# Four sequence pairs moved into the steps of the prompt attention in a two-layer hybrid decoder step

## The chip, the cores and the metric

One launch of one program on one core of a Trainium2 chip. The metric is the device time of one execution, from the first to the last instruction and what lies around it, in microseconds (us). The engines are TensorE (PE, with its weight loads PEld), VectorE (DVE), ScalarE (ACT), GpSimd (POOL) and SyncE (SP), which only issues transfers here. Each engine works through its own queue in program order; they meet at semaphores. All arithmetic around this change is f32, which PE does in two instructions per product.

## The reference, cut to what matters

A two-layer decoder handles a prompt (512 tokens) and eight short sample sequences (8 tokens each) with the same weights. In each layer the normed input goes through one projection into three head groups: RG-LRU, MLA (attention over a compressed latent) and GLA. Each group's output is normed by itself, the three are concatenated, multiplied by `w_out` and added to the input; a mixture of experts follows. The prompt attends to itself; each sample sequence attends to 1024 cached positions, kept in 8 pages of 128, and to its own 8 tokens:

```
past_ckv = cache_ckv[l][page_table].reshape(nb, -1, KV_RANK)       # 128 columns
past_kpe = cache_kpe[l][page_table].reshape(nb, -1, QK_ROPE)       # 32 columns
s = (einsum('bqhr,bkr->bhqk', qa, ckv) + einsum('bqhr,bkr->bhqk', qp, kpe)) * scale
p = softmax(where(k_pos <= q_pos, s, -inf))
o = einsum('bhqk,bkr->bqhr', p, ckv)
...
merged = concatenate([rmsnorm(out_a, n_a), rmsnorm(out_b, n_b), rmsnorm(out_c, n_c)], axis=-1)
return merged @ lw['w_out'], ...
```

## The kernel before, in words

Every engine has a program of its own in one block; loops over layers and steps are unrolled in Python, and the five programs are written so that their queues fit together. PSUM has eight banks; `psum_plan` lists every use of a bank in PE's order, and the uses go round the eight banks in turn. `begin` makes PE wait until the use eight places earlier has been read, `take` makes a reader wait until the bank is full, `give` marks it read and `after` waits for that mark.

**The prompt attention** runs in `ATT_STEPS` = 35 steps, one per head and query tile (8 x 4), with three more to drain. In a step PE makes the scores of tile `s`, transposes the probabilities of tile `s - 2` (`pt`), and every eighth step multiplies a pair of heads with the values (`pv`) and spreads their reciprocal sums (`rs`). DVE takes the maximum of the scores, ACT the exponential and the copies of the transposes. In the same steps the GLA group runs: five state products (`delta`, steps 0 to 6), the products between chunks (`inter`, step 7), and 16 offset sums (`dp` and `ds`, steps 8 to 24), whose factors DVE multiplies and whose results it adds up. At step 26 (`GN_STEP`) follow the sums of the GLA norm, and at step 27 DVE finishes the GLA output (`out_c`, L1335 to L1340).

**The sample attention** takes the eight sequences in four pairs, each on 128 rows (2 sequences x 8 heads x 8 tokens). A pair has three pieces in PE's queue. `sample_scores` (L1662, L1666, L1671) makes the scores over 1088 columns in three banks (`ss`); DVE takes the maximum (`sample_max`, L1286) and ACT the exponentials (`sample_exp`, L875); DVE divides by the sum over all 1088 columns (`sample_divide`, L1295). `sample_values` transposes the probabilities (L1682, L1684; banks `sp`), waits for ACT's three copies (L882, L885) and multiplies them with the cached latent (L1692, L1695; bank `sv`). `sample_turn` (L1701) transposes the copied result (`svt`), which ACT puts into `qas`. Pair 0 has its pieces in steps 27, 30 and 33. Pairs 1 to 3 follow after the last step in the order of `SAMPLE_ORDER`. When all four are turned, PE multiplies by `w_uv` (`uvs`, L1798).

**The pages.** SP loads them (L486 to L503). For each pair it reads sixteen page numbers into registers, then issues one transfer of 192 KB a page: per partition 128 latent columns, 128 transposed ones and 128 for the transposed rotary key, of which only 32 partitions hold data. There are two buffers in `rg`. Pair 0's load waits for `inter` and for the GLA states to be stored, pair 1's for `out_c`, whose inputs lie under its buffer, and pairs 2 and 3 for the values of pair 0 and 1. The halves of `w_out` are issued on the same queue between them.

**The norm of the groups** follows `out_b`, the mark that the MLA output is complete: ACT squares the eight 128-row pieces of the three groups (L967), PE sums them over partitions with a matrix of ones (`osum`, L1807), ACT makes the reciprocal roots through Ln and Exp (`rstds`, L758 and L761, a table load each), and DVE multiplies (L1355, `merged`). The output projection (`wo`, L1818) takes the eight pieces in order; DVE adds its result to `x` (L1361). Norm, router and the experts (L1858 to L1887) follow. SP loads the first expert's weights after the merge (L514, L518).

The functions, with their lines:

Of the kernel before, what the change touches and what calls it, by code (L numbers as in the profile page):

```python
# [17 lines left out]
ALU = mybir.AluOpType  # L18
ACT = mybir.ActivationFunctionType
# [3 lines left out]
P = 128  # L23
# [30 lines left out]
ATT_STEPS = HEADS * 4 + 3  # L54
# [90 lines left out]
def psum_plan():  # L145
# [19 lines left out]
    for s in range(ATT_STEPS):  # L165
# [9 lines left out]
        if s == SAMPLE_STEP:  # L175
            keys += [("ss", 0, k) for k in range(3)]
        if s == SAMPLE_STEP + 3:
            keys += [("sp", 0, k) for k in range(3)] + [("sv", 0)]
        if s == SAMPLE_STEP + 6:
            keys += [("svt", 0)]  # L180
# [7 lines left out]
    for kind, p in SAMPLE_ORDER:  # L188
        keys += {"scores": [("ss", p, k) for k in range(3)],
                 "values": [("sp", p, k) for k in range(3)] + [("sv", p)], "turn": [("svt", p)]}[kind]  # L190
    keys += [("uvs",)]
    keys += [("osum", k, h) for k in range(3) for h in range(2)]
# [7 lines left out]
def hybrid_step(nc, a, o):  # L200
# [5 lines left out]
    with ExitStack() as ctx:  # L206
# [36 lines left out]
        def cut(region, at, *dims):  # L243
# [14 lines left out]
        wout = [cut(rb, 0, KT, 512), cut(ra, 0, KT, 512)]  # L258
# [19 lines left out]
        spread = cut(rb, 1152, SEQ)  # L278
# [30 lines left out]
        pg = [cut(rg, 6144 * k, 2, NPAGE, 3 * P) for k in (1, 0)]  # L309
        CKV, CKVT, KPET = slice(0, P), slice(P, 2 * P), slice(2 * P, 3 * P)  # L310
        sprob = cut(re, 8960, 1088)
        spT = cut(re, 10048, 9, P)
        osq = cut(rg, 0, 8, T)
        ors = cut(rg, 4608, 3, T)
# [17 lines left out]
            gmsk_ready kt_ready diff_ready exp_ready w_ready gn_ready out_c max_ready rs_ready s_max s_prob  # L332
# [6 lines left out]
        page_in = [sem(f"page{k}_in") for k in range(2)]  # L339
        wout_in = [sem(f"wout{k}_in") for k in range(2)]  # L340
# [101 lines left out]
        def _(sp):  # L442
# [16 lines left out]
            for L in range(DEPTH):  # L459
# [60 lines left out]
                sp.wait_ge(S["merged"], 8 * (L + 1))  # L520
# [209 lines left out]
        def _(act):  # L730
# [62 lines left out]
            for L in range(DEPTH):  # L793
# [77 lines left out]
                def sample_exp(p):  # L871
                    act.wait_ge(S["s_max"], 4 * L + p + 1)
                    for k, (at, n) in enumerate(((0, 512), (512, 512), (1024, NS))):
                        bk = take(act, L, ("ss", p, k))
                        give(fn(sprob[:, at:at + n], bk[:, 0:n], ACT.Exp, bias=sm[:, 84:85],  # L875
                                accum_out=sm[:, 85 + k:86 + k]), ("ss", p, k))

                def probabilities_out(p):
                    for k in range(3):
# [4 lines left out]
                        else:  # L884
                            give(copy(spT[:NS, 8, :], bk[:NS, 0:P]), ("sp", p, k))  # L885

                def sample_rows(p):
                    bk = take(act, L, ("sv", p))
                    give(copy(svs[:, p % 2, :], bk[:, 0:P]), ("sv", p))
# [4 lines left out]

                for s in range(ATT_STEPS):
# [26 lines left out]
                    if s == 1:  # L923
# [6 lines left out]
                        for e in range(2):  # L930
                            bk = take(act, L, ("qp", e))
                            give(copy(qp[0:ROPE, :, :].rearrange("p b (h e q) -> p e h b q", e=2, q=NQ)[:, e],
# [7 lines left out]
                    if s == SAMPLE_STEP + 1:  # L940
                        sample_exp(0)
# [1052 lines left out]
```

## Time and profile before

| | |
|---|---|
| median of 3 runs | 1611.6 us (1609.57 to 1612.38) |
| the profiled execution | 1611.4 us |
| its span | 1609.5 us |
| mean granted TensorE clock | 0.888 |
| PE busy | 1275.7 us, 79% |
| DVE, ACT, POOL busy | 545.7, 359.1, 320.8 us |
| HBM read, written | 289.96, 27.09 MB |

Rows are read so. A timeline row has its start and length in us, the engine, the line, the operation, what it writes and reads, and how many instructions are merged in it; brackets hold idle time before it and what ended it.
### The profile page before, as it was taken

To read this page: it belongs to the slowest core of one execution; us is meant where nothing else is said; L and a number is where in the kernel's file an instruction comes from. 1 tells how busy PE (TensorE), PEld (TensorE's weight loads), DVE (VectorE), ACT (ScalarE), POOL (GpSimd) and SP (SyncE) were. 2 spreads that over 40 slices of the span, in tenths; PEclk is the share of its full clock that TensorE was granted. 3 is DMA by queue.
4 is the path that set the end of the run, shared out by engine and by line. 5 is a ranking of instruction groups with operands and counts; after the bars stand their busy time and mean duration, and the time that the engine had idled before them with its cause. 6 is when DMAs were issued, how large, how long until landed. Compare 5 with 4: busy or idle time off the path is not lost.

```text
span 1609.5 us, 21838 instructions
## 1 busy us (share of the span) xinstructions
PE 1275.7 (79%) x7203; PEld 767.7 (48%) x7204; DVE 545.7 (34%) x1345; ACT 359.1 (22%) x823; POOL 320.8 (20%) x729
## 2 busy tenths in 40 slices
PE   5999977769956887778499997866898477888881
PEld 4777555434453443444277765533446244444440
DVE  2275685102243111111516557731113411111115
ACT  4233336121111101111314333522311011011112
POOL 0012410000002333333102052000000133333440
PEclk9999999669957999999699999975897599999996
DMA  5310021442094889995521002064207499978745
GB/s 211 99 36 27 9 80 45 165 144 78 40 385 168 344 348 400 408 407 227 197 97 63 27 0 88 1 205 136 92 13 286 175 381 408 377 275 344 292 174 182
DMA packets 98900, 299.11 MB, mean 186 GB/s; under 512 B 13230, under 2 KB 29966, under 8 KB 98450
## 3 DMA queue, kind: packets, MB, share of 16 engines
q1 hardware_dynamic: 85426, 273.21, 45.3%
q0 software_dynamic: 13408, 25.04, 4.3%
q8 instruction: 39, 0.64, 0.2%
q14 instruction: 27, 0.22, 0.0%
HBM read 289.96 MB, written 27.09 MB: 197 GB/s over the span
## 4 chain that ended last, share of the span: by engine, by line
PE 52%; DMA 22%; DVE 11%; issue 6%; SPq 4%; ACT 2%; POOL 2%; POOLq 1%; DVEq 0%; ACTq 0%
DMA ra<-h_rows,slot_now 19%; PE bank L1542 14%; PE bank L1818 9%; PE bank L1876 5%; PE bank L1887 3%; PE bank L1858 3%; SPq L495 2%; PE bank L1831 2%; PE bank L1574 2%; DVE rg L1262 1%; PE bank L1740 1%; PE bank L1662 1%; PE bank L1666 1%; PE bank L1807 1%; DVE rf L1259 1%
## 5 line engine op out<-in xcount | busy, mean ns | idle before, releaser
L1542 PE MATMUL bank<-ra,rb 128*128 128x288 f32 (+1 forms) x896 | 225.2, 414 | 1.9 <-ACT ra L736 1.9
L1542 PEld LDWEIGHTS bank<-ra,rb 128*128 128x128 f32 (+1 forms) x896 | 170.4, 191 | 54.0 <-issue 3.6
L1477 DVE COPY rb<-bank 128x512 f32<-128x512 f32 x71 | 49.1, 692 | 223.0 <-DMA y_rows<-rb,home_now 158.1
L990 ACT ACTIVATE rb<-bank 128x128 f32<-128x128 f32 x71 | 19.7, 278 | 417.9 <-PE bank L1876 417.9
L1858 PE MATMUL bank<-cst,ra 128*128 128x128 f32 x292 | 49.7, 295 | 74.3 <-DMA ra<-h_rows,slot_now 74.2
L1876 PE MATMUL bank<-rg,rb 128*64 128x256 f32 x768 | 92.3, 395 | 8.0 <-issue 5.2
L1887 PE MATMUL bank<-re,rb 128*64 128x512 f32 x296 | 81.5, 677 | 14.2 <-DVE rb L1473 14.2
L1471 DVE TENSOR_TENSOR rb<-rb,bank 128x128 f32<-128x128 f32 x71 | 20.4, 288 | 196.8 <-ACT rb L990 196.8
L1876 PE MATMUL bank<-re,rb 128*64 128x256 f32 x736 | 84.8, 383 | 2.5 <-issue 0.8
L697 POOL DMA_INDIRECT ra<-h_rows,slot_now x73 | 77.1, 1056 | 39.7 <-issue 39.7
L1876 PEld LDWEIGHTS bank<-rg,rb 128*64 128x64 f32 x768 | 56.7, 142 | 53.2 <-issue 29.2
L1858 PEld LDWEIGHTS bank<-cst,ra 128*128 128x128 f32 x292 | 31.8, 145 | 105.3 <-DMA ra<-h_rows,slot_now 98.0
L686 POOL DMA_INDIRECT y_rows<-rb,home_now x71 | 73.0, 1029 | 38.8 <-issue 38.8
L1876 PEld LDWEIGHTS bank<-re,rb 128*64 128x64 f32 x736 | 53.1, 138 | 44.6 <-issue 22.6
L982 ACT COPY rb<-bank 128x512 f32<-128x512 f32 x73 | 42.8, 586 | 140.0 <-PE bank L1858 140.0
L671 POOL DMA_DIRECT2D h_rows<-re x4 | 2.2, 550 | 353.8 <-DVE re L1008 353.8
L1740 PE MATMUL bank<-re 128*128 128x128 f32 (+3 forms) x128 | 52.1, 490 | 9.4 <-DVE rf L1259 6.8
L1887 PE MATMUL bank<-rg,rb 128*64 128x512 f32 x192 | 48.2, 624 | 9.2 <-DVE rb L1473 9.2
L1876 PE MATMUL bank<-rf,rb 128*64 128x256 f32 x448 | 51.3, 382 | 1.4 <-issue 1.2
L1361 DVE TENSOR_TENSOR x<-x,bank 128x512 f32<-128x512 f32 (+1 forms) x20 | 13.7, 686 | 109.9 <-PE bank L1818 109.9
L918 ACT ACTIVATE re<-bank,sm 128x128 f32<-128x128 f32 (+1 forms) x64 | 33.9, 530 | 73.9 <-DVE sm L1303 73.6
L1637 PE MATMUL bank<-re,cst 128*128 128x512 f32 (+15 forms) x128 | 40.5, 434 | 11.6 <-DVE rf L1259 6.3
(354 smaller groups left out, 2055.6 us busy)
## 6 DMA issues: line engine op xcount, KB each, us to landing
rg<-in_w_moe SPq DMA_DIRECT2D x24, 2048.0 KB, 11.3
re<-in_w_moe SPq DMA_DIRECT2D x20, 2048.0 KB, 13.0
re<-in_w_moe SPq DMA_DIRECT2D x30, 1024.0 KB, 15.0
rg<-in_cache SPq DMA_DIRECT2D x128, 192.0 KB, 3.5
rg<-in_w_moe SPq DMA_DIRECT2D x24, 1024.0 KB, 13.7
rf<-in_w_moe SPq DMA_DIRECT2D x10, 2048.0 KB, 12.4
ra<-in_w_moe SPq DMA_DIRECT2D x10, 2048.0 KB, 13.4
rb<-in_win SPq DMA_DIRECT2D x28, 512.0 KB, 3.8
```

Of the source, the lines that this page charges most:

```text
L686: nc.gpsimd.indirect_dma_start(y_halves, bass.IndirectOffsetOnAxis(ap=home_now[:, 0:1], axis=0), ysb, None, bounds_check=4 * T - 1, oob_is ...
L697: nc.gpsimd.indirect_dma_start(xg, None, h_halves, bass.IndirectOffsetOnAxis(ap=slot_now[:, 0:1], axis=0), bounds_check=2 * T - 1, oob_is_ ...
L918: give(fn(prob[:, s % 2, 0:n], bk[:, 0:n], ACT.Exp, bias=peaks[:, s % 16:s % 16 + 1], accum_out=sums[:, s % 16:s % 16 + 1]), key)
L982: copy(xT, bank[0][:, :].rearrange("p (k h n) -> p k h n", k=4, h=2)).then_inc(S["xt_ready"], 1)
L1477: V.tensor_copy(ysb, bank[5][:, :]).then_inc(S["y_ready"], 1)
L1542: ins = mm(bk[:mrows, 0:HALF], win[:, n % 4, k, :mrows], hT[:, k, cols], start=k == 0, stop=k == KT - 1)
L1637: done(mm(bk[:, 0:n], cst[:, C_BM + j * P:C_BM + (j + 1) * P], gw[:, d % 2, 0:n], start=True, stop=True), ("dp", d, j))
L1740: mm(bk[:, 0:n], qt[:, hd, i * P:n], kt[:, hd, 0:n], start=True, stop=False)
L1818: ins = mm(bk[:r, :], merged[k][:, t * P:t * P + r], wout[n][:, k, :], start=k == 0, stop=k == 7)
L1858: ins = tr(bank[0][:, k * P:(k + 1) * P], xg[:, k * P:(k + 1) * P], ident)
L1876: ins = mm(bank[2][SLOTS * h:SLOTS * (h + 1), 0:DE], xT[:, k % 4, k // 4, :], wgu[s][:, k, h * DE:(h + 1) * DE], start=k == 0, stop=k == K ...
L1887: ins = mm(bank[5][SLOTS * n:SLOTS * (n + 1), :], actT[:, k, :], wdn[s][:, k, 512 * n:512 * n + 512], start=k == 0, stop=k == 1)
```

## The change

All four pairs run inside the steps, now 36: scores at steps 14, 19, 24 and 29, values three steps later, the turn six steps later. The exponentials are no longer divided; DVE multiplies the 128 columns of the `sv` bank by the reciprocal sum instead (ACT copied them before). A page is 128 KB (latent and transposed latent) with the rotary key as a second transfer of 16 KB into `kpg`, pair `p` on partitions 32p to 32p + 31; `qp` is made on all 128 partitions so that the scores can use those rows. The buffers lie over other memory: pair 0 and 2 in `rg`, 1 and 3 in `rb`, and pair 1 no longer waits for `out_c`. `w_out`'s first half goes to `rg` after `out_c`, and the first expert's load after the fifth output tile. The RG-LRU and GLA groups are squared at step 30, summed at 31, their roots taken at 32 and multiplied at 33; the MLA group alone is normed after `out_b`. The output projection takes pieces 0, 1, 6, 7 first.

```
-ATT_STEPS = HEADS * 4 + 3
+ATT_STEPS = HEADS * 4 + 4
-SAMPLE_STEP = 27
-SAMPLE_ORDER = (("scores", 1), ("scores", 2), ("values", 1), ("values", 2), ("turn", 1), ("turn", 2),
-                ("scores", 3), ("values", 3), ("turn", 3))
+SAMPLE_AT = (14, 19, 24, 29)
+EARLY_STEP = 30
+MERGE_ORDER = (0, 1, 6, 7, 2, 3, 4, 5)
+NORM_GROUPS = {0: (0, 2, 256), 2: (2, 4, 256), 1: (4, 8, 512)}
...
-        wout = [cut(rb, 0, KT, 512), cut(ra, 0, KT, 512)]
+        wout = [cut(rg, 0, KT, 512), cut(ra, 0, KT, 512)]
-        spread = cut(rb, 1152, SEQ)
+        spread = cut(re, 13568, SEQ)
-        pg = [cut(rg, 6144 * k, 2, NPAGE, 3 * P) for k in (1, 0)]
-        sprob = cut(re, 8960, 1088)
-        spT = cut(re, 10048, 9, P)
-        osq = cut(rg, 0, 8, T)
-        ors = cut(rg, 4608, 3, T)
+        pg = [cut(rg, 4096, 2, NPAGE, 2 * P), cut(rb, 0, 2, NPAGE, 2 * P)]
+        kpg = cut(rg, 8192, 2, NPAGE, P)
+        sprob, sprob_new = cut(rg, 10240, 1024), cut(re, 2944, NS)
+        spT, spT_new = cut(rg, 11264, 8, P), cut(re, 3008, P)
+        osq = cut(rg, 4096, 8, T)
+        ors = cut(re, 8960, 3, T)
...
 SP
-                take(sp, L, ("inter", 2))
-                sp.wait_ge(S["gla_out"], 32 * (L + 1))
                 for p in range(4):
                     page = [sp.value_load(pages[0:1, col:col + 1], ...) for col in ...]
-                    if p == 1:
-                        sp.wait_ge(S["out_c"], L + 1)
+                    if p == 0:
+                        take(sp, L, ("inter", 2))
+                        sp.wait_ge(S["gla_out"], 32 * (L + 1))
                     if p > 1:
                         take(sp, L, ("sv", p - 2))
                     for n in range(2 * NPAGE):
                         sp.dma_start(pg[p % 2][:, n // NPAGE, n % NPAGE, :], a["cache"][...])
-                    if p == 2:
-                        after(sp, L, ("pv", 3))
-                        sp.dma_start(wout[0], wo_rows[:, :, 0:512]).then_inc(wout_in[0], 16)
-                    if p == 3:
-                        take(sp, L, ("pv", 3))
-                        sp.dma_start(wout[1], wo_rows[:, :, 512:1024]).then_inc(wout_in[1], 16)
+                        sp.dma_start(kpg[ROPE * p:ROPE * (p + 1), n // NPAGE, n % NPAGE, :], a["cache_kpe"][...])
+                sp.wait_ge(S["out_c"], L + 1)
+                sp.dma_start(wout[0], wo_rows[:, :, 0:512]).then_inc(wout_in[0], 16)
+                take(sp, L, ("pv", 3))
+                sp.dma_start(wout[1], wo_rows[:, :, 512:1024]).then_inc(wout_in[1], 16)
...
-                sp.wait_ge(S["merged"], 8 * (L + 1))
+                take(sp, L, ("wo", 0, TT - 1))
                 load_gate_up(0, 0)
...
 ACT
+                    for p, at in enumerate(SAMPLE_AT):
+                        if s == at + 1:
+                            if p == 0:
+                                act.wait_ge(S["gla_out"], 32 * (L + 1))
+                            sample_exp(p)
+                        if s == at + 3:
+                            probabilities_out(p)
+                        if s == at + 6:
+                            sample_out(p)
+                    if s == EARLY_STEP:
+                        act.wait_ge(S["out_c"], L + 1)
+                        for p in range(3):
+                            take(act, L, ("sv", p))
+                        squares(range(0, 4))
+                    if s == EARLY_STEP + 2:
+                        group_rstds(0, 2)
...
-                for k in range(8):
-                    fn(osq[:, k, :], merged[k], ACT.Square).then_inc(S["osq_ready"], 1)
-                rstds(L, *[(("osum", k, h), ors[:, k, cols], n, "ors_ready")
-                           for k, n in enumerate((256, 512, 256)) for h, cols in enumerate(halves)])
+                squares(range(4, 8))
+                group_rstds(1)
...
 DVE
-                    link(V.reciprocal(sm[:, 89:90], sm[:, 88:89]))
-                    V.tensor_scalar(sprob, sprob, sm[:, 89:90], None, ALU.mult).then_inc(S["s_prob"], 1)
+                    V.reciprocal(sm[:, 89:90], sm[:, 88:89]).then_inc(S["s_sums"], 1)
+                def sample_rows(p):
+                    bk = take(dve, L, ("sv", p))
+                    dve.wait_ge(S["s_sums"], 4 * L + p + 1)
+                    give(V.tensor_scalar(svs[:, p % 2, :], bk[:, 0:P], sm[:, 89:90], None, ALU.mult), ("sv", p))
+                def normed_groups(slots, ready):
+                    dve.wait_ge(S["ors_ready"], 6 * L + ready)
+                    for n in slots:
+                        k, g = MERGE_ORDER[n], (0, 0, 2, 2, 1, 1, 1, 1)[n]
+                        V.scalar_tensor_tensor(merged[k], ...).then_inc(S["merged"], 1)
...
+                        if s == at: sample_max(p)
+                        if s == at + 1: sample_divide(p)
+                        if s == at + 4: sample_rows(p)
+                    if s == EARLY_STEP + 3:
+                        normed_groups(range(0, 4), 4)
...
 PE
+                    pe.wait_ge(kpage_in[p % 2], 16 * 2 * NPAGE * (2 * L + p // 2 + 1))
+                    rows = slice(ROPE * p, ROPE * (p + 1))
-                            ins = mm(bk[64 * b2:64 * b2 + 64, 0:n], qp[0:32, 2 * p + b2, :],
-                                     pg[p % 2][0:32, b2, 4 * k:4 * k + 4, KPET] if k < 2 else kpeT[0:32, SEQ:T],
+                            ins = mm(bk[64 * b2:64 * b2 + 64, 0:n], qp[rows, 2 * p + b2, :],
+                                     kpg[rows, b2, 4 * k:4 * k + 4, :] if k < 2 else kpeT[rows, SEQ:T],
-                    pe.wait_ge(S["s_prob"], 4 * L + p + 1)
+                    for k in range(3):
+                        after(pe, L, ("ss", p, k))
...
+                        if s == at: sample_scores(p)
+                        if s == at + 3: sample_values(p)
+                        if s == at + 6: sample_turn(p)
...
+                    if s == EARLY_STEP + 1:
+                        for g in (0, 2):
+                            group_sums(g)
...
+                group_sums(1)
...
-                        for k in range(8):
+                        for i, k in enumerate(MERGE_ORDER):
                             if n == 0 and t == 0:
-                                pe.wait_ge(S["merged"], 8 * L + k + 1)
+                                pe.wait_ge(S["merged"], 8 * L + i + 1)
```

## Rows read from the trace of the kernel before

**Rows 1.** Windows, layer 0: steps 14 to 34, pairs 1 to 3, group norm.
```profile
224.80:292.50 67.70, 53.24 (x398) 37.30 (x400) 40.84 (x120) 32.88 (x89) 3.52 (x8) 0.90 0.15 48
292.50:354.80 62.30, 40.19 (x222) 19.88 (x218) 9.28 (x22) 11.27 (x34) 0.00 (x0) 0.62 0.51 169
354.80:372.10 17.30, 11.69 (x48) 8.41 (x48) 1.47 (x4) 11.85 (x22) 0.00 (x0) 0.80 0.09 31
```

**Rows 2.** Waits, 170 to 372 us: engine, line, releaser, total us, times, longest.
```profile
PE bank L1662 <- DMA rg<-in_cache: 15.0, 2, 7.8
```

**Rows 3.** Line L495, both layers: issue ns min/median/max, waits for it, landing.
```profile
L495 SPq DMA_DIRECT2D rg<-in_cache x128: 332/333/1891, 202.3 to 1105.8; - x128
...
  PE bank L1662: 29.2, 4
...
DMA to landing us min/median/max: 2.3/3.5/6.1
```

**Rows 4.** Timeline, layer 0: last `rs`, last turn, `uvs`.
```profile
291.74 1.07 PE L1752 MATMUL bank<-cst,sm 128*64 128x128 f32 x16
...
353.99 0.33 PE L1701 MATMUL bank<-cst,rf 128*128 128x128 f32 x1 [0.37 <-ACT rf L889]
...
354.87 0.69 PE L1798 MATMUL bank<-re 128*64 128x64 f32 x16 [0.56 <-ACT re L893]
```

**Rows 5.** Timeline: pair 0's scores, an exponential, pair 2's transposes and values.
```profile
264.53 1.08 PE L1662 MATMUL bank<-rg,re 128*64 128x512 f32 x4
...
269.08 0.22 PE L1671 MATMUL bank<-mask 128*64 128x64 bf16 x2
...
297.86 0.69 ACT L875 ACTIVATE re<-bank,sm 128x512 f32<-128x512 f32 x1 [4.42 <-DVE sm L1288]
...
321.00 1.87 PE L1682 MATMUL bank<-cst,re 128*128 128x128 f32 x8
...
325.80 0.44 PE L1695 MATMUL bank<-re 64*64 64x128 f32 x4
```

**Rows 6.** Timeline: step 29's scores, GLA output, pair 0's values.
```profile
269.95 0.60 PE L1740 MATMUL bank<-re 128*128 128x256 f32 x2
...
272.90 1.36 DVE L1340 SCALAR_TENSOR_TENSOR rf<-rf,rg 128x1152 f32<-128x1152 f32 x1
...
278.02 1.97 PE L1682 MATMUL bank<-cst,re 128*128 128x128 f32 x8 [1.81 <-DVE re L1295]
...
284.65 0.63 PE L1695 MATMUL bank<-re 64*64 64x128 f32 x4
```

**Rows 7.** Windows of PE alone: busy, granted clock, DMA share, GB/s.
```profile
282.00:285.00 3.00, 3.00 (x30) 0.50 0.93 294
```

**Rows 8.** Timeline, layer 0: `out_b`, group norm, first output product and its add.
```profile
356.06 0.15 DVE L1349 COPY sm<-sm 128x1 f32<-128x1 f32 x1
...
360.95 1.28 ACT L758 ACT_TABLE_LOAD   x1
...
371.21 1.55 DVE L1355 SCALAR_TENSOR_TENSOR rf<-rf,vec,rg 128x576 f32<-128x576 f32 x2 [15.00 <-ACT rg L761]
...
373.96 3.60 PE L1818 MATMUL bank<-rb,re 128*128 128x512 f32 x8
...
379.32 0.69 DVE L1361 TENSOR_TENSOR x<-x,bank 128x512 f32<-128x512 f32 x1 [2.19 <-PE bank L1818]
```

**Rows 9.** The chain that ended last: start, us, engine and line.
```profile
35.98 39.00 PE bank L1542 x160
```

**Rows 10.** Timeline: `inter`, then the issues of pairs 0 and 1, and 2.
```profile
187.75 4.84 PE L1629 MATMUL bank<-rg 128*64 128x32 f32 x160
...
202.31 80.98 SPq L495 DMA_DIRECT2D rg<-in_cache  x32
...
292.28 9.27 SPq L495 DMA_DIRECT2D rg<-in_cache  x16
```

**Rows 11.** Timeline: the first expert's first products, layer 0.
```profile
500.13 5.13 PE L1876 MATMUL bank<-rg,rb 128*64 128x256 f32 x30 [0.86 <-ACT rb L982]
```

More of the change, by code:

```diff
@@ L187, in psum_plan @@
             keys += [("gnorm", j, h) for j in range(2) for h in range(2)]
[L188 to L190 removed]
+        if s == EARLY_STEP + 1:
+            keys += [("osum", g, h) for g in (0, 2) for h in range(2)]
     keys += [("uvs",)]
[L192 removed]
+    keys += [("osum", 1, h) for h in range(2)]
     keys += [("wo", n, t) for n in range(2) for t in range(TT)]
@@ L872, in sample_exp @@
                     act.wait_ge(S["s_max"], 4 * L + p + 1)
-                    for k, (at, n) in enumerate(((0, 512), (512, 512), (1024, NS))):
+                    for k, dst in enumerate((sprob[:, 0:512], sprob[:, 512:1024], sprob_new)):
                         bk = take(act, L, ("ss", p, k))
-                        give(fn(sprob[:, at:at + n], bk[:, 0:n], ACT.Exp, bias=sm[:, 84:85],
+                        give(fn(dst, bk[:, 0:512 if k < 2 else NS], ACT.Exp, bias=sm[:, 84:85],
                                 accum_out=sm[:, 85 + k:86 + k]), ("ss", p, k))
@@ L884, in probabilities_out @@
                         else:
[L885 to L889, printed above, removed]
+                            give(copy(spT_new[:NS, :], bk[:NS, 0:P]), ("sp", p, k))
                 def sample_out(p):
@@ L893, in sample_out, with squares, group_rstds @@
                     give(copy(qas[:, 2 * p:2 * p + 2, :], bk[:, 0:P].rearrange("p (b c) -> p b c", b=2)), ("svt", p))
+                def squares(slots):
+                    for n in slots:
+                        fn(osq[:, n, :], merged[MERGE_ORDER[n]], ACT.Square).then_inc(S["osq_ready"], 1)
+                def group_rstds(*groups):
+                    rstds(L, *[(("osum", g, h), ors[:, g, cols], NORM_GROUPS[g][2], "ors_ready")
+                               for g in groups for h, cols in enumerate(halves)])
                 for s in range(ATT_STEPS):
@@ L1721, in sample_queries, with group_sums @@
                         for n in range(4):
-                            ins = mm(bk[0:ROPE, n * NS:(n + 1) * NS], sel[rows, 0:ROPE], qt[rows, 2 * n + e, SEQ:T],
+                            ins = mm(bk[:, n * NS:(n + 1) * NS], sel[rows, :], qt[rows, 2 * n + e, SEQ:T],
                                      start=True, stop=True)
                         done(ins, ("qp", e))
+                def group_sums(g):
+                    n0, n1, _ = NORM_GROUPS[g]
+                    pe.wait_ge(S["osq_ready"], 8 * L + n1)
+                    for h, cols in enumerate(halves):
+                        bk = begin(pe, L, ("osum", g, h))
+                        for n in range(n0, n1):
+                            ins = mm(bk[:, 0:HALF], ones, osq[:, n, cols], start=n == n0, stop=n == n1 - 1)
+                        done(ins, ("osum", g, h))
                 pe.wait_ge(S["uv_in"], 16 * (L + 1))
@@ L1789, in _ @@
                         gla_norm_sums()
-                for kind, p in SAMPLE_ORDER:
-                    {"scores": sample_scores, "values": sample_values, "turn": sample_turn}[kind](p)
+                    if s == EARLY_STEP + 1:
+                        for g in (0, 2):
+                            group_sums(g)
                 for p in range(4):
@@ L1800, in _ @@
                 done(ins, ("uvs",))
-                for g, (k0, k1) in enumerate(((0, 2), (2, 6), (6, 8))):
-                    pe.wait_ge(S["osq_ready"], 8 * L + k1)
-                    for h, cols in enumerate(halves):
-                        bk = begin(pe, L, ("osum", g, h))
-                        for k in range(k0, k1):
-                            ins = mm(bk[:, 0:HALF], ones, osq[:, k, cols], start=k == k0, stop=k == k1 - 1)
-                        done(ins, ("osum", g, h))
+                group_sums(1)
                 for n in range(2):
```

106 lines of the change are left out of this document (44 added, 62 removed).

## The prediction, before the changed kernel ran

> **What bounds the kernel now.** I read the page's slices first: TensorE is busy nearly everywhere, but in a stretch near 300 us, and again in the second layer, its granted clock drops well below full. The windows by stage say why [rows 1]. The prompt attention's steps 14 to 34 (224.8 to 292.5 us) keep PE 53.2 of 67.7 us busy at 0.90. The next 62.3 us, in which sequence pairs 1 to 3 run one after another, have 40.2 us of PE at a clock of 0.62, that is, mostly at 1.2 GHz. The 17.3 us after them are the norm of the three head groups. Together that is 80 us a layer in which the reader should see no engine full. The waits name the two ends: PE stands 15.0 us for cache pages in two waits [rows 2], and the line that issues the pages has four such waits over both layers, 29.2 us, so the second layer behaves as the first [rows 3]. The rest of the stretch is each pair's own chain (scores, maximum, exponentials, transposes, copies, values, turn) with nothing beside it.
>
> I work on layer 0 and double it. The execution profiled took 1611.4 us (span 1609.5); the median of the runs is 1611.6, so I subtract from 1611.4.
>
> **What leaves.** From the end of the last `rs` product (291.74 + 1.07 = 292.81) to the start of `uvs` (354.87) there are 62.1 us [rows 4]. Afterwards only pair 3's turn, its copy and the hand-over stay there: 353.99 to 354.87, 0.9 us. So 61.2 us leave.
>
> **What enters the steps.** A pair's price on PE at 2.4 GHz: scores 264.53 to 269.30, 4.8 us; transposes, three ACT copies and values 321.00 to 326.24, 5.2 us; the turn 0.3 [rows 5]. That is 10.3 us, all in PE's queue, since `sample_values` waits for its copies where it stands. Pairs 0 and 1 whole and pair 2's scores come ahead of step 27: 2 x 10.3 + 4.8 = 25.4. After it come the rest of pair 2 (5.5) and pair 3 (10.3); pair 0, which stood there, goes: 4.8 for its scores, 278.02 to 285.28 for its values [rows 6] and 0.3, 12.4 in all. Net 25.4 + 15.8 - 12.4 = 28.8.
>
> Two corrections of opposite sign I take as equal. PE is idle 14.5 us in the stretch [rows 1], mostly waiting for DVE's GLA sums, and can swallow some of the pair work. Against that, a step with scores uses seven or eight of the eight PSUM banks, so the next step's offset sums wait until ACT has read the three score banks, behind that step's prompt exponential; ACT needs 0.7 us for a 512-column one [rows 5] and the read of its sum, some 2 us for three, once per pair. DVE gets three maxima of the same columns, about as long, in steps where it is the fullest engine; its normalising of `sprob` leaves, and a small scaled copy of the `sv` bank comes. Bounds: all of the idle time absorbed, less 4 us of such waits, -10; every moved pair at its price in the tail, (62.1 - 15.0) / 3 = 15.7 instead of 10.3, +16. I stay at the PE price, because the queue is in order and the row is of the same instructions.
>
> The early norm adds on PE four matmul pairs for each of two groups. 160 matmul instructions of the same 288 columns take 39.0 us, 0.244 each [rows 9]; a product is two of them, so 8 products are 3.9 us. On ACT four squares, two table loads, four Ln and four Exp stand ahead of the copy of `pt` 31, for which the last `pv` waits: I charge 3.3 us of wait (0 if PE's own values of pair 3 cover it, 8 if they cover none). Steps in all: 28.8 + 3.9 + 3.3 = 36.0.
>
> The table load's row shows 1.28 us [rows 8]. The Trainium skill (ScalarE: Activation LUTs, What ACT_TABLE_LOAD costs) counts a drain with each switch, about 2.66 us together; the change adds two switches a layer, so by that rule it would be up to 2.8 us a layer more and 1560 us in the end. The eight squares before the load run from 356.21 to 360.95, 0.59 each, which leaves no visible drain; I go by the row.
>
> **The tail.** From `out_b` (356.06 + 0.15) to DVE's first add after the first output product (379.32) are 23.1 us [rows 8]. After the change: four squares 2.4 (0.59 each); the sums of group 1, 16 instructions at 0.244, 3.9 [rows 9]; an Ln, a table load of 1.28 and two Exp, together some 2.7; one DVE product 0.8 (two in 1.55). Meanwhile PE does the four products of the early groups (0.9 each from eight instructions in 3.60) in its queue behind the sums, and after DVE's first product has the other four left: 3.6. Sum 13.4, so 9.7 leave.
>
> Per layer at full clock: -61.2 + 36.0 - 9.7 = -34.9.
>
> **The clock.** Before, PE stopped while DVE made the GLA norm (272.90 + 1.36), and the values that followed at 278.02 ran at 1.2 GHz [rows 6, 7]. That DVE work and ACT's table loads stay at steps 26 and 27, so the stop stays, and now pair 2's values and perhaps pair 3's scores follow it: 2 us, or 6 with the scores. A second such stop is likely at the end, where PE waits for ACT's early norm, then for `out_b`: pv, rs and the group sums at half clock cost up to 7. I take 3 + 3. Net -28.9 per layer, -58 for both: 1611.4 - 58 = 1553.6, **1554 us**.
>
> **Edits that I cost at nothing.** SP: pair 0's sixteen page numbers are now read ahead of the wait for `inter`, so issues start near 192.6 rather than 202.31 [rows 10]. A pair now takes 32 issues instead of 16. One issue takes 0.33 us of SP [rows 3], 16 in a row 9.27 us, 0.58 each, paced by the data [rows 10]; reading 16 page numbers 9.7 us (192.59 to 202.31). At 0.58, the upper end, pair 1's pages are issued by 239.5, pair 2's by 267.8 and pair 3's by 296.1, plus 3.5 to land [rows 3]: 299.6. Pair 3's scores stand in step 29, at 269.95 before [rows 6]; ahead of them come 25.4 and pair 2's values (5.2), less pair 0's old scores (4.8), and what the clock and the waits add: 296 to 302. So it is close at that pace, and well early at 0.40, where pair 3's issue waits for pair 1's values instead. A late pair would hold in PE's queue all prompt steps from 29 on. `out_c`, `wout` and the gain come after on SP: `wout[0]` now waits for `out_c`, not for `pv` 3, and is there before the output product. The first expert's load waits for the fifth output tile instead of the merge, some 15 us later against the stage; its first reader starts at 500.13 [rows 11], over 100 us on; nothing if that cover stays. The other expert loads follow the same point as before. The other new waits are met when they come: ACT's at step 30 for `out_c` and `sv` 0 to 2 (PE made `sv` 2 three steps earlier; behind it stand the copies of `pt` 29 on, for which PE would wait), ACT's for `gla_out` at step 15 and DVE's for its own reciprocal. Page bytes fall from 192 to 144 KB. Moving `spread`, `sprob`, `osq` and `ors`, and `qp` on 128 partitions, change no operation's length.
>
> **Rivals.** *The idle time takes it in.* If the DVE-bound steps swallow the pairs to the lower bound and the clock holds: -34.9 - 10 + 2 = -43 a layer, 1525. For it: 14.5 us of PE idle. Against: in-order waits within a step, at every pair. *The pairs cost in the steps what they cost in the tail* (15.7 each, half clock after each wait): -34.9 + 16 + 6 = -13 a layer, 1586. For it: pair 0's values took 7.3 us within the steps [rows 6]. Against: that was after the norm's stop alone. *SP becomes the bound, slower than before.* Pair 3's pages land at 192.6 + 128 c + 3 x 9.7 + 3.5 for c us an issue; at c = 0.60 PE begins to wait, and at 0.82 the whole gain of 28.9 is gone; at 1.0, 1656. For it: the longest single issue took 1.89 us [rows 3]. Against: the median of 0.33, and 0.58 with larger transfers. The Trainium skill (DMA: Bandwidth & Descriptors, Bandwidth) speaks against splitting: it calls transfers under 64 KB descriptor-dominated, and its table gives 0.68 us at 4 KB and 0.95 at 64 KB; with about 0.8 for the 16 KB ones and 0.4 for the pages, c would be some 0.6, an estimate, at the edge of that loss. No row here shows a 16 KB load. *Nothing moves:* the steps stretch by all that the tail loses; only with both upper bounds at once.
>
> **Chances.** The forecast, 1544 to 1570, has 0.50; the first rival, below 1544, 0.24; the second, 1570 to 1600, 0.18; SP 0.05; no change 0.03. A measurement of this kernel tells 0.2% (3 us) from no change, so faster 0.92, same 0.03, slower 0.05. From 1530 to 1586 about 0.8 lie.
>
> **What would show it.** Right: no DMA releaser for the scores; `uvs` about 1.2 us after the last turn's start; step 27's first score 25 us after its old place; the last `rs` near 329 to 335; the first DVE add after the output product near 350; the clock at 0.5 after the GLA norm. Wrong, towards slower: PE waiting for `in_cache` ahead of pair 3's scores, or SP's 32 issues taking over 19 us. Wrong, towards faster: steps 14 to 26 stretched by under 18 us.

## The result, and the profile after

The changed kernel took 1566.2 us (median of four runs), the kernel before 1612.0 beside it: ratio 0.972, 95% interval 0.967 to 0.977. That is 46 us faster; the prediction was 1554, so 58 faster. The four times lie on two levels, 1560 and 1572, and the execution profiled (1572.1, span 1570.2, 39.3 below the span before) is one of the upper ones. In a later group of runs the same kernel took 1577.7 beside 1610.5 (`after_again` below), 33 us faster, so the size of the gain is known only as some 33 to 46 us.

The forecast of the prediction, per layer, was -28.9. From the start of `inter` (187.75 before [rows 10], 187.06 after) to the first add of the output product (379.32 [rows 8], 359.14) the way is 191.6 us before and 172.1 after in layer 0, 191.4 and 172.1 in layer 1: 19.4 us a layer are saved, 9.5 fewer than forecast. All that the change moved lies in this way, since two layers of it make 38.8 of the 39.3 us.

First, the windows of the stages, answering to [rows 1]: the steps up to step 27, the other steps with what is left of the pairs, and the group norm (columns: stretch, length, busy time of PE, its weight loads, DVE, ACT, POOL, granted clock, DMA share, GB/s).

```profile
224.10:300.20 76.10, 60.70 (x409) 36.93 (x410) 37.66 (x121) 26.95 (x79) 3.57 (x8) 0.87 0.31 87
300.20:339.80 39.60, 28.07 (x225) 19.49 (x223) 12.96 (x24) 22.04 (x53) 0.00 (x0) 0.91 0.15 54
339.80:355.40 15.60, 11.58 (x43) 7.10 (x41) 2.14 (x5) 7.50 (x12) 0.00 (x0) 0.78 0.48 169
```

The 62 us at a clock of 0.62 are gone. What stays is PE's own work at about 0.9, with stops in it. PE's waits from `inter` to the first add no longer name a DMA, in either layer; three of the longest (engine, line, releaser: us, times, longest) are the copies of a pair's probabilities, the squares of the early norm and DVE's read of a pair's values:

```profile
PE bank L1703 <- ACT re L888: 8.0, 3, 4.4
PE bank L1743 <- ACT rg L897: 6.1, 2, 3.1
...
PE bank L1645 <- DVE rf L1298: 3.4, 1, 3.4
```

The steps up to step 27, in PE's timeline (start, length, engine, line, operation, idle before it and its releaser), with step 27's first score last. In the kernel before that score stood at 263.30:

```profile
263.30 1.02 PE L1740 MATMUL bank<-re 128*128 128x512 f32 x2
```

In the changed kernel:

```profile
256.94 0.59 PE L1645 MATMUL bank<-re,cst 128*128 128x192 f32 x2 [3.40 <-DVE rf L1298]
...
278.10 0.55 PE L1766 MATMUL bank<-cst,re 128*128 128x128 f32 x3 [1.57 <-DVE rf L1298]
...
278.64 1.50 PE L1672 MATMUL bank<-rg,re 128*64 128x512 f32 x4
...
280.07 1.97 PE L1676 MATMUL bank<-rg,re 32*64 32x512 f32 x4
...
300.18 1.02 PE L1760 MATMUL bank<-re 128*128 128x512 f32 x2
```

L1298 is `sample_rows`, which the change moved from ACT to DVE, last in DVE's step. PE stands 3.40 us for it in step 18 (in the kernel before, 1.52 us at that place, for an offset product) and 1.57 us in step 24. Right behind the second stop pair 2's scores run at 1.97 us for four products instead of 1.08. The windows of PE alone show it as the clock (length, busy, granted clock, DMA share, GB/s):

```profile
276.00:279.00 3.00, 1.43 (x10) 1.00 0.49 135
279.00:282.00 3.00, 3.00 (x10) 0.53 0.50 145
...
288.00:291.00 3.00, 2.04 (x8) 0.50 0.44 129
```

Then the end of the layer's attention: pair 2's values behind the GLA norm, pair 3's scores, the early sums, the values of pair 3, the last `rs`, `uvs`, the last group's sums, and on DVE `out_b` and the first add.

```profile
306.87 3.42 PE L1703 MATMUL bank<-rg 128*64 128x128 f32 x32 [4.40 <-ACT re L888]
312.32 1.08 PE L1672 MATMUL bank<-rb,re 128*64 128x512 f32 x4
322.35 5.84 PE L1743 MATMUL bank<-rg,cst 128*128 128x288 f32 x16 [2.99 <-ACT rg L897]
332.17 1.97 PE L1703 MATMUL bank<-rb,rg 128*64 128x128 f32 x32 [2.67 <-ACT re L761]
338.77 1.07 PE L1772 MATMUL bank<-cst,sm 128*64 128x128 f32 x16
340.88 0.69 PE L1819 MATMUL bank<-re 128*64 128x64 f32 x16 [0.79 <-ACT re L892]
...
342.06 0.15 DVE L1361 COPY sm<-sm 128x1 f32<-128x1 f32 x1
344.70 7.17 PE L1743 MATMUL bank<-rg,cst 128*128 128x288 f32 x16 [3.13 <-ACT rg L897]
...
359.14 0.69 DVE L1369 TENSOR_TENSOR x<-x,bank 128x512 f32<-128x512 f32 x1 [1.60 <-PE bank L1833]
```

And SP: the first issues of pair 3's pages, and its last. Issues follow each other by 0.52 us in the median, whether they carry 128 KB (L497) or 16 KB (L500). The last is out 21 us before pair 3's scores.

```profile
274.75 0.33 SPq L497 DMA_DIRECT2D rb<-in_cache  x1
275.27 0.33 SPq L500 DMA_DIRECT2D rg<-in_cache_kpe  x1
...
291.10 0.33 SPq L500 DMA_DIRECT2D rg<-in_cache_kpe  x1
```

### The profile page after: what moved, and what is told of

It reads as the page before. It is cut to its first block, busy times and chain, and to the rows that moved or that the text cites. A ratio compares the mean times of both kernels' runs of the same rounds, so it can differ in the third digit from the quotient of the medians.

```text
span 1570.2 us, 22262 instructions
## 1 busy us (share of the span) xinstructions
PE 1257.3 (80%) x7203; PEld 762.4 (49%) x7204; DVE 542.6 (35%) x1345; ACT 359.2 (23%) x819; POOL 320.4 (20%) x729
## 4 chain that ended last, share of the span: by engine, by line
PE 55%; DMA 22%; DVE 9%; issue 6%; ACT 5%; POOL 2%; POOLq 1%; SPq 0%; DVEq 0%; ACTq 0%
DMA ra<-h_rows,slot_now 20%; PE bank L1550 14%; PE bank L1833 8%; PE bank L1891 5%; PE bank L1873 3%; PE bank L1902 3%; PE bank L1760 2%; PE bank L1846 2%; PE bank L1582 2%; PE bank L1743 2%; PE bank L1676 1%; PE bank L1672 1%; PE bank L1782 1%; PE bank L1645 1%; DVE x L1492 1%
## 5 line engine op out<-in xcount | busy, mean ns | idle before, releaser
L989 ACT ACTIVATE rb<-bank 128x128 f32<-128x128 f32 x71 | 19.7, 277 | 413.5 <-PE bank L1891 413.5
L1479 DVE TENSOR_TENSOR rb<-rb,bank 128x128 f32<-128x128 f32 x71 | 20.5, 288 | 200.7 <-ACT rb L989 200.7
L1902 PE MATMUL bank<-re,rb 128*64 128x512 f32 x296 | 76.1, 637 | 14.2 <-DVE rb L1481 14.2
L1645 PE MATMUL bank<-re,cst 128*128 128x512 f32 (+15 forms) x128 | 44.0, 465 | 17.5 <-DVE rf L1298 6.8
L1313 DVE TENSOR_REDUCE sm<-bank 128x1 f32<-128x128 f32 (+1 forms) x64 | 31.0, 489 | 56.3 <-PE bank L1761 55.6
```

Of the source, the lines that this page charges most:

```text
L1645: done(mm(bk[:, 0:n], cst[:, C_BM + j * P:C_BM + (j + 1) * P], gw[:, d % 2, 0:n], start=True, stop=True), ("dp", d, j))
L1902: ins = mm(bank[5][SLOTS * n:SLOTS * (n + 1), :], actT[:, k, :], wdn[s][:, k, 512 * n:512 * n + 512], start=k == 0, stop=k == 1)
```

## The experiments

Twelve runs in four groups of kernels; the kernels of a group ran on one chip beside the kernel before (1610 to 1611 us each time). Times are medians of four runs (five for `rows_late_norm`).

| kernel | us | ratio to before, 95% |
|---|---|---|
| after_again | 1577.7 | 0.9785 to 0.9825 |
| rows_first | 1551.2 | 0.9620 to 0.9672 |
| late_norm | 1569.2 | 0.9693 to 0.9803 |
| split_pages | 1671.3 | 1.0332 to 1.0395 |
| rows_again | 1553.5 | 0.9630 to 0.9662 |
| rows_late_norm | 1550.5 | 0.9603 to 0.9635 |
| rows_two_in_tail | 1546.5 | 0.9578 to 0.9611 |
| rows_at_23_28 | 1557.8 | 0.9647 to 0.9693 |
| two_again | 1547.5 | 0.9597 to 0.9629 |
| three_in_tail | 1598.8 | 0.9917 to 0.9954 |
| tail_early_sums | 1552.0 | 0.9610 to 0.9646 |
| pair1_read_first | 1564.2 | 0.9647 to 0.9750 |

### after_again: the changed kernel once more

> The changed kernel once more, unchanged. Theory (the clock): the two levels of its time, 1560 and 1572 us, are executions in which TensorE keeps or loses its clock during pair 2's scores, steps 24 to 27. Times again near 1560 or 1572; in an execution near 1560 the eight long products of pair 2's scores take 1.08 us instead of 1.98 us in at least one layer, and steps 24 to 27 take 18 to 20 us there instead of 24.2. Rival: the levels come from somewhere else (the expert stages), and steps 24 to 27 take 24 us in either.

All four times were 1576 to 1581, above both levels expected, so no execution near 1560 came with a profile, and where the two levels differ could not be read directly. The interval of this run does not meet that of the first (0.967 to 0.977): the same kernel differs by 0.9% between them, and why is not shown. In the profile pair 2's scores are at half speed in both layers again (the two big score banks start at 281.23 and 284.56 in layer 0, 3.3 us apart where 2.0 is full clock). It serves as the base of the next three.

### rows_first: DVE reads the pair's values early in its step

```diff
+                    if s - 4 in SAMPLE_AT:
+                        sample_rows(SAMPLE_AT.index(s - 4))
                     if s > 0 and s % 8 == 0:
...
-                        if s == at + 4:
-                            sample_rows(p)
```

> VectorE scales and reads a pair's values (the bank sv) right after the step's maximum, ahead of the product with the row sums and the GLA offset. Theory (bank waits): the offset sums of step 18 wait 3.40 us, and a transpose of step 24 1.57 us, for this read alone; both waits go, some 5 us a layer, so 1556 us, and where the waits also took the clock in pair 2's scores, up to 12 us more (1544). Rival: the step's end was set by ScalarE's copies and exponentials anyway, so PE waits the same time for them: within 3 us of the changed kernel (1560 to 1572).

1551.2 us, 26.5 below the changed kernel on the same chip (15 below its first result). The rival is refuted. Of the two waits the first became 1.53 us (for an offset product's read of its own bank, as in the kernel before), the second 0.16. Pair 2's scores keep full clock:

```profile
256.25 1.13 PE L1760 MATMUL bank<-re 128*128 128x512 f32 x2 [1.53 <-DVE rf L1258]
...
275.68 0.55 PE L1766 MATMUL bank<-cst,re 128*128 128x128 f32 x3 [0.16 <-DVE rf L1298]
276.31 1.08 PE L1672 MATMUL bank<-rg,re 128*64 128x512 f32 x4
...
291.23 1.02 PE L1760 MATMUL bank<-re 128*128 128x512 f32 x2
```

```profile
279.00:282.00 3.00, 3.00 (x23) 1.00 0.53 146
```

Step 27's first score comes at 291.23 instead of 300.18; with `inter` 0.94 later here, that is 9.9 us in layer 0. The waits themselves account for 3.4 + 1.6 - 1.5 - 0.2 = 3.3 of it, so the larger part is the clock behind them: from `inter` to that score PE was busy 90.9 us in the changed kernel and 83.2 us here, with the same work.

### late_norm and rows_late_norm: the early norm undone

```diff
-                    if s == EARLY_STEP:
...
-                        squares(range(0, 4))
-                    if s == EARLY_STEP + 2:
-                        group_rstds(0, 2)
...
-                squares(range(4, 8))
-                group_rstds(1)
+                squares(range(0, 8))
+                group_rstds(0, 2, 1)
```

(PE's sums and DVE's products likewise go behind `out_b`.)

> The two early head groups are squared, summed and normed after out_b again, with the third. Theory of the prediction: the steps lose 3.9 us of sums and 3.3 us of waits for ScalarE, and the stretch from out_b to the first add grows from 16.9 us (as traced) by 9.7 us; net 2.5 us a layer slower, 1571 us. Rival: the early norm costs more than it gives, since in the trace it shows 5.84 us of sums and 2.99 + 2.67 us of waits against a gain of 23.1 - 16.9 = 6.2 us; then 5.3 us a layer faster, 1556 us.

1569.2 us, but with runs from 1563 to 1580 against 1576 to 1581 for its base: too wide to price 5 us. So it was made again on `rows_first`, where the clock in the steps is steady.

> rows_first with the two early head groups normed after out_b, with the third: the price of the early norm where the clock is steady. By the prediction's terms (7.2 us of sums and waits in the steps, 9.7 us taken from the tail) it is 2.5 us a layer slower than rows_first, 1556 us. Rival: the early norm costs PE 3.0 + 5.7 + 2.7 = 11.4 us in the steps, as rows_first's trace has them, and gives 6 to 7 us in the tail: 4 to 5 us a layer faster, 1542 us.

1550.5 beside 1553.5: neither the 5 us slower of the prediction nor the 9 us faster of the rival; the intervals overlap. The traces show why. These are the last `rs` products, `out_b` and the first add with the early norm (`rows_again`):

```profile
333.87 1.07 PE L1772 MATMUL bank<-cst,sm 128*64 128x128 f32 x16
...
337.16 0.15 DVE L1361 COPY sm<-sm 128x1 f32<-128x1 f32 x1
...
352.67 0.69 DVE L1369 TENSOR_TENSOR x<-x,bank 128x512 f32<-128x512 f32 x1 [1.61 <-PE bank L1833]
```

and without it (`rows_late_norm`, where `inter` stood 0.11 us earlier):

```profile
326.59 1.07 PE L1762 MATMUL bank<-cst,sm 128*64 128x128 f32 x16
...
329.88 0.15 DVE L1350 COPY sm<-sm 128x1 f32<-128x1 f32 x1
...
352.29 0.69 DVE L1359 TENSOR_TENSOR x<-x,bank 128x512 f32<-128x512 f32 x1 [3.63 <-PE bank L1821]
```

In layer 0 the early norm holds the last `rs` up by 7.2 us and shortens the way from `out_b` to the add by 22.4 - 15.5 = 6.9 us; in layer 1 the two are 8.6 and 6.9. It is worth nothing, within what these runs can tell.

### split_pages: twice as many issues for the same bytes

```diff
-                        sp.dma_start(pg[p % 2][:, n // NPAGE, n % NPAGE, :], ...
...
+                        for c in range(2):
+                            sp.dma_start(pg[p % 2][:, n // NPAGE, n % NPAGE, c * P:(c + 1) * P], ...
...
+                            sp.dma_start(kpg[ROPE * p + 16 * c:ROPE * p + 16 * c + 16, ...
```

> Every page transfer is cut into two, so 64 issues on SP for each pair instead of 32; the bytes are the same. Theory (the issues themselves cost 0.52 us each, whatever they carry): a pair's pages take 33 us, the last of pair 3's is issued near 353 us instead of 291 and its scores wait 40 us for it: 80 us more in two layers, 1640 to 1656 us (the prediction's own price for 1.0 us an issue was 1656). Rival: the cadence is set by what a transfer carries, half the bytes take half the time, nothing waits: 1560 to 1572 us.

1671.3 us, 94 above its base, somewhat over the theory's 80. The starts of pair 0's 64 issues run from 195.36 to 229.46, 0.54 us apart (0.52 in the median) with half the bytes: the cadence belongs to the issue. PE then waits for the pages of pairs 1, 2 and 3, and the scores behind each wait are at half clock, which the theory had not counted:

```profile
PE bank L1673 <- DMA rg<-in_cache_kpe: 32.0, 3, 16.7
```

```profile
319.38 1.97 PE L1673 MATMUL bank<-rg,re 128*64 128x512 f32 x4 [16.72 <-DMA rg<-in_cache_kpe]
```

So the prediction's slower rival is a real mechanism, with a price near its own (1656 at 1.0 us an issue of the change; two issues of 0.54 are 1.08), but the change stays clear of it at 0.52.

### rows_again, rows_two_in_tail, two_again: does the place of the pairs matter?

> rows_first once more, as the base of the three kernels beside it. Theory: without VectorE's late read TensorE keeps its clock through steps 24 to 27 in every execution, so the time stays near 1551 us (1549 to 1557) and shows no level 12 us apart. Rival: the clock falls there in some executions all the same, and times near 1565 us appear.

1552.3 to 1555.1 in four runs, one level.

```diff
-SAMPLE_AT = (14, 19, 24, 29)
+SAMPLE_AT = (14, 19)
+TAIL_ORDER = (("scores", 2), ("scores", 3), ("values", 2), ("values", 3), ("turn", 2), ("turn", 3))
```

> rows_late_norm with pairs 2 and 3 behind the last step, interleaved as the kernel before had its pairs 1 and 2; their pages lie ready long before. By the prediction's prices (10.3 us a pair in the steps, 15.7 us in the tail) two pairs moved out are 10.8 us a layer slower than rows_late_norm: 22 us more, 1564 to 1578 us. Rival (a pair costs in the steps what it costs in the tail): within 4 us of rows_late_norm. Rival (idle time absorbs part of a pair in the steps): more than 30 us slower.

1546.5 us, 4 below `rows_late_norm`. The prediction's prices (22 us slower) are refuted, and with them the idea that idle time in the steps absorbs a pair; the first rival, the same cost in either place, holds. The same kernel once more:

> rows_two_in_tail once more, as the base of the two kernels beside it: 1544 to 1549 us if its gain over the kernels with all pairs in the steps holds, 1550 us and more if it was chance.

1547.5, ratio 0.9613 against 0.9619 for `rows_late_norm` and 0.9646 for `rows_again`: the same as with all pairs in the steps and the norm late, or a few us better. In two_again's trace the two pairs run between the last `rs` and `uvs` in 19.7 us, at full clock (the two rows, then the window):

```profile
301.22 1.07 PE L1779 MATMUL bank<-cst,sm 128*64 128x128 f32 x16
...
321.67 0.69 PE L1826 MATMUL bank<-re 128*64 128x64 f32 x16 [0.56 <-ACT re L894]
```

```profile
302.00:321.70 19.70, 16.97 (x152) 8.66 (x149) 5.32 (x15) 6.94 (x21) 0.00 (x0) 1.00 0.31 108
```

That is 9.8 us a pair, behind the steps, with nothing beside them but each other. The prediction had 15.7 for this place, a mean over the kernel before, where the pairs ran at 0.62.

### three_in_tail: the wait for pages brought back

```diff
-SAMPLE_AT = (14, 19)
-TAIL_ORDER = (("scores", 2), ("scores", 3), ("values", 2), ("values", 3), ("turn", 2), ("turn", 3))
+SAMPLE_AT = (14,)
+TAIL_ORDER = (("scores", 1), ("scores", 2), ("values", 1), ("values", 2), ("turn", 1), ("turn", 2),
+              ("scores", 3), ("values", 3), ("turn", 3))
```

> rows_two_in_tail with pair 1 behind the last step too, in the order that the kernel before had. Theory (what the change removed is the wait for pages and its clock, not the place): with two page buffers pair 3's pages are asked for when pair 1's values are done, in the tail; 32 issues of 0.52 us and 2 us of landing, less 5 us of pair 2's values and turns, leave PE waiting 12 to 15 us, and pair 3's scores then run at half clock, 4 to 6 us longer: 16 to 21 us a layer more, 1578 to 1589 us. Rival (pairs simply cost more in the tail, or less): a move of one pair at 10.2 us for 10.3 us, within 4 us of rows_two_in_tail, or 5.4 us a layer slower (1557 us) by the prediction's prices.

1598.8 us, 51.3 above its base (`two_again`): the theory's mechanism, larger than it said. Only one pair went to another place, at a like price of its own, but its values now come in the tail, so pair 3's pages are asked for there. The wait equals the sum of the two in the kernel before [rows 2], and all of pair 3 behind it runs at 1.2 GHz (waits, then the windows of wait and pair):

```profile
PE bank L1686 <- DMA rb<-in_cache: 15.0, 1, 15.0
```

```profile
312.00:326.80 14.80, 0.00 (x0) 0.03 (x1) 0.00 (x0) 0.15 (x1) 0.00 (x0) 0.62 0.49 133
326.80:346.70 19.90, 15.63 (x72) 7.40 (x72) 2.43 (x7) 3.34 (x10) 0.00 (x0) 0.50 0.57 210
```

In layer 0, 15.0 of wait and 19.9 - 9.8 = 10.1 of slower pair are 25 us; twice that is the 51 us. Of the 10.1, some 7 are the clock (PE busy 15.6 us for this pair, 17.0 for the two in `two_again`); the rest is idle time, since pair 3 has no other pair beside it.

### rows_at_23_28: pairs 2 and 3 a step earlier

```diff
-SAMPLE_AT = (14, 19, 24, 29)
+SAMPLE_AT = (14, 19, 23, 28)
```

> rows_first with pair 2 begun at step 23 and pair 3 at step 28 instead of 24 and 29. Theory: PE's 4.40 us stop ahead of pair 2's values is ScalarE's Ln, Exp and two table loads of the GLA norm in the same step; a step earlier the values are past before them and pair 3's scores (5.3 us of PE) run beside them: 4 to 5 us a layer faster, 1541 to 1543 us. Rival: the prompt's transposes wait for the same ScalarE work, the stop only changes its line: 1549 to 1553 us.

1557.8 us, 4 slower than `rows_again`, with intervals that overlap: both missed. The stop ahead of pair 2's values shrank to 0.97, but pair 3's values now came one step after the early norm's squares and waited for copies that ACT made behind them, and the last `pv` waited for a `pt` copy behind the early Ln and Exp:

```profile
316.26 3.60 PE L1703 MATMUL bank<-rb,rg 128*64 128x128 f32 x32 [4.82 <-ACT re L888]
331.50 4.54 PE L1782 MATMUL bank<-ra 128*64 128x128 f32 x40 [6.43 <-ACT ra L919]
```

### tail_early_sums: the early sums into the tail

```diff
+                act.wait_ge(S["out_c"], L + 1)
+                squares(range(0, 4))
                 sample_exp(2)
...
                     {"scores": sample_scores, "values": sample_values, "turn": sample_turn}[kind](p)
+                    if (kind, p) == ("values", 3):
+                        for g in (0, 2):
+                            group_sums(g)
```

> rows_two_in_tail with the squares of the two early groups on ScalarE at the start of the tail, where it idles, and their sums on PE behind pair 3's values; Ln and Exp stay after out_b. Theory: 2.4 us of squares and 3.9 us of sums leave the chain from out_b to the first product, 3.9 us of sums enter PE's work ahead of it, and the four Ln of these groups no longer follow the sums: 2 to 4 us a layer faster, 1538 to 1543 us. Rival: the chain behind out_b is Ln, Exp and VectorE's products, the sums were hidden in it: 0 to 4 us a layer slower, 1546 to 1555 us.

1552.0 us, 4.5 slower than `two_again`, with intervals that just overlap: the theory missed, and the time is the rival's. In layer 0 the way from `out_b` to the add went from 24.1 us (322.85 to 346.96) to 22.5 (327.83 to 350.29), a gain of 1.7. The way from the start of the last `rs` to `uvs`, in which the sums now stand, went from 20.5 us (301.22 to 321.67) to 24.0 (302.67 to 326.65), a loss of 3.5.

### pair1_read_first: which of the two stops takes the clock?

```diff
+                    if s == SAMPLE_AT[1] + 4:
+                        sample_rows(1)
...
-                        if s == at + 4:
+                        if s == at + 4 and p != 1:
                             sample_rows(p)
```

> The changed kernel with VectorE's early read for pair 1 alone (step 23); pair 0's read at step 18 stays behind the GLA offset. It parts the two stops. Theory A (the 1.57 us stop right ahead of pair 2's scores is what takes the clock): the stop goes, pair 2's scores run at 1.08 us for each four products, 7 us a layer are saved, 1552 to 1562 us. Theory B (the 3.40 us stop of step 18 is needed too, with the shorter ones behind it): the clock still falls to 0.50 near pair 2's scores, 1 to 2 us a layer are saved, 1563 to 1575 us. In both the 3.40 us wait at step 18 stays.

1564.2 us, from 1557.7 to 1570.2, again on two levels 12 us apart. Neither theory fits. In layer 0 the clock fell already at the 3.39 us stop of step 18, and pair 1's scores ran at half clock; pair 2's then ran at full clock:

```profile
259.23 0.59 PE L1647 MATMUL bank<-re,cst 128*128 128x192 f32 x2 [3.39 <-DVE rf L1298]
...
261.10 1.98 PE L1674 MATMUL bank<-rb,re 128*64 128x512 f32 x4
...
286.52 1.08 PE L1674 MATMUL bank<-rg,re 128*64 128x512 f32 x4
```

In layer 1 of the same execution no scores were slow, with the same 3.39 us stop at step 18. With the 1.57 us stop gone pair 2's scores were slow in neither layer. So the long stop of step 18 can take the clock by itself, but does not in each layer. That fits times on two levels; that the levels of the changed kernel are such falls is not shown, since no execution of the lower level was profiled.

## Why the prediction was right, and where not

**The total (1554 us).** The first result, 1566.2, lies in the range of 1544 to 1570, at its upper end, and that is in part luck: the same kernel later took 1577.7, which is outside. In the profiled execution the change saves 19.4 us a layer where 28.9 was forecast. One step of the sum makes up that difference.

**What leaves (61.2 us).** Right. No DMA releases PE any more, and `uvs` follows the last turn by 1.1 us (forecast 1.2).

**What enters ahead of step 27 (25.4, with the two corrections taken as equal).** This is the step that failed. The score stands 300.18 - 263.30 + 0.69 = 37.6 us later. The prediction named the mechanism, a bank held until another engine has read it, and set at most 4 us for ACT's exponentials. It mentioned DVE's "small scaled copy of the `sv` bank" and gave it no price. What counted was not its length (0.35 us) but its place, behind the row-sum product and the GLA offset in DVE's step. PE's offset sums needed that bank. With the read moved forward the score stands 27.7 us later (291.23, `inter` at 188.00), and the forecast of the whole holds: 161.9 us from `inter` to the first add in layer 0 and 163.3 in layer 1, a saving of 29.6 and 28.1 where 28.9 was forecast; its span is 62 us below the one before (forecast 58). Two smaller misses cancel in it: 2.3 us too few ahead of step 27, and some 3.7 too many behind it, where the steps up to the end of the last `rs` grew by 10.0 us, 3.1 of them the clock, instead of by 10.6 and the clock. Which term of the 10.6 was too large is not shown.

A reading of the rows behind the two corrections was wrong too. Of the 14.5 us in which PE was idle [rows 1], the waits of the kernel before name DVE's GLA products and sums for 6.5, not for most; 4.0 was one wait for ACT's exponentials of pair 0.

**The clock (+3 +3).** Right where the forecast put it, and short of one fall. Behind the 4.40 us stop at the GLA norm pair 2's values took 3.4 us instead of the 1.9 of pair 3's; pair 3's scores, which the forecast left open, ran at 1.08. At the end the early sums took 5.7 us and the last group's 7.0, instead of 3.9 each (the next rows start at 328.02 and 351.71). Together these are 6.4 us, and 6.1 in `rows_first`. The fall that the forecast did not have is the one at pair 2's scores, behind DVE's read: 6.6 us in layer 0 (the 9.9 us that `rows_first` saves there less the 3.3 of waits).

**The early norm (7.2 in the steps, -9.7 in the tail).** In the steps it cost 7.2 and 8.6 us in the two layers. The first agrees in its sum and not in its parts: in `rows_again` the early sums alone took 7.0 us, at a clock of 0.50, where 3.9 was forecast. The tail gave 6.9. Without the early norm it is 22.4 us, not 23.1, and with it 15.5, not 13.4; 1.5 of that is the clock again (the last group's 16 sum instructions took 5.4 us instead of 3.9). So the early norm costs 0.3 and 1.7 us a layer where a gain of 2.5 was forecast.

**The pairs' prices (10.3 in the steps, 15.7 in the tail).** The first was somewhat low, the second much too high. From `rows_late_norm` to `two_again` the way from `inter` to the last `rs` shrinks by 24.8 and 24.0 us: 12 us a pair in the steps, with the stops that it brings. In the tail a pair costs 9.8 us without a page wait. The 15.7 was a mean at a clock of 0.62 with idle time in it, and the prediction drew its bound and its second rival from it. So the place counts for little: the two profiled executions lie 14.5 us apart, but the medians of the kernels only 3 to 4. The wait for pages and the clock that PE lost by it count for much more, 25 us in layer 0 of `three_in_tail` against `two_again`, and 51 of the 63 us between `two_again` and the kernel before. That an earlier load alone, with the pairs left behind the steps, would give the same is argued from this; no run has it, and none has a third page buffer.

**The rivals.** SP at 0.52 us an issue stayed under the 0.60 at which PE would wait; the small transfers cost nothing else that shows in PE's waits. The prediction called the 0.58 us of the kernel before, at 192 KB, paced by the data; that is not shown, and from 128 KB down the pace was 0.52 us whatever the size. The estimate of 0.6 from the table of the Trainium skill (DMA: Bandwidth & Descriptors, Bandwidth) was too high, by the trace. A table load took 1.28 us again, started at 344.67 where the squares ahead of it ended (342.25 + 2.40), and another, from 352.43 to 353.71, was followed by the exponentials at 353.72. The drain that the Trainium skill (ScalarE: Activation LUTs, What ACT_TABLE_LOAD costs) counts with each switch did not show here.

Better than both kernels are `rows_first` (DVE's read moved, 1551 to 1553 us) and, with the norm late and pairs 2 and 3 behind the steps, `rows_two_in_tail` (1546 to 1548).

## What to carry to other kernels

When work moves to another engine, price the bank that it releases and the place in that engine's step, not the length of the instruction: a read of 0.35 us held PE for 3.4, where 1.5 remained with the read moved forward. Before a stage is moved beside another one, ask which of its costs are a wait and the half clock behind it; if an earlier load takes those away, the move itself may be worth nothing. A price per piece taken from a stretch at a clock of 0.62 is not the price of that piece at full clock: 15.7 us against 9.8 here.

## What the hardware showed unexpectedly

The clock fell behind stops much shorter than the 15 us wait for pages, and the length of the last stop does not tell whether it falls. In the changed kernel it went to 0.53 and 0.50 right behind a stop of 1.57 us (step 24), while the windows behind the 3.40 us stop of step 18 show 1.00. In `pair1_read_first` the scores behind the like stop of 3.39 us took 1.98 us for four products in one layer and 1.08 in the other. In `rows_first` stops of 1.53 to 1.87 us between 252 and 294 us left it at 1.00, but behind one of 1.94 us in step 17 pair 0's values ran at half clock:

```profile
244.99 2.79 PE L1703 MATMUL bank<-rg 128*64 128x128 f32 x32 [1.94 <-ACT re L888]
```

```profile
246.00:249.00 3.00, 3.00 (x24) 0.50 0.00 0
```

The kernel before has 0.59 from 228 to 231 us, and from 219 us on it had no stop longer than 0.55 us. SP's issues followed each other by 0.52 us in the median for 128 KB, 64 KB, 16 KB and 8 KB alike.
